# Experts of a mixture layer in plain fp32 on 32-column tiles of the array, instead of three fp32r products of split operands

## The reference, cut to what matters

```python
def swiglu(h, w_gu, w_down):
    gt, up = jnp.split(h @ w_gu, 2, axis=-1)
    return (jax.nn.silu(gt) * up) @ w_down

def moe(h, w_r, b_r, w_gu, w_down):
    t = h.reshape(-1, shp[-1])
    logits = (t @ w_r).astype(jnp.float32) + b_r.astype(jnp.float32)
    top_v, top_i = lax.top_k(logits, TOP_K)
    wts = jax.nn.softmax(top_v, axis=-1)
    comb = jnp.sum(jax.nn.one_hot(top_i, N_EXPERTS, dtype=jnp.float32) * wts[..., None], axis=1)
    for e in range(N_EXPERTS):
        out = out + comb[:, e:e + 1] * swiglu(t, w_gu[e], w_down[e])
```

## Time and profile before

| | us |
|---|---|
| median of 3 runs | 1981.36 (1981.35 to 1981.62) |
| the profiled execution | 1976.57 |
| its span | 1974.4 |
| first product of expert 0 to the end of expert 7 in it | 942.2 to 1950.1 |

### The profile page before, as it was taken

The page is one execution under the profiler, slowest core; times in us unless marked ns, Lnnn a source line. Parts: engine busy times, 40 slices in busy tenths (PEclk is TensorE's granted clock), DMA queues, the critical chain, the costliest instruction groups (busy, mean ns, idle before and its releaser), DMA issues.

```text
span 1974.4 us, 33543 instructions
## 1 busy us (share of the span) xinstructions
PE 1923.0 (97%) x12982; PEld 1627.6 (82%) x12982; DVE 1565.5 (79%) x2210; ACT 1135.9 (58%) x1385; POOL 239.6 (12%) x279
## 2 busy tenths in 40 slices
PE   7999999999998999999999999999999999999997
PEld 3778998899997778988888888888888888888885
DVE  5896457655674976287999989989899898998995
ACT  2214344545432243344777877877778777777774
POOL 2550422000006332340000000000000000000000
PEclk9999999999999999999999999999999999999998
DMA  9576345555552664444799999999999999999993
GB/s 351 186 285 236 131 159 181 196 181 182 179 174 69 203 222 141 167 150 153 269 363 365 353 323 349 368 359 357 324 342 363 365 352 343 334 363 371 345 346 119
DMA packets 143063, 524.12 MB, mean 265 GB/s; under 512 B 16192, under 2 KB 16704, under 8 KB 142272
## 3 DMA queue, kind: packets, MB, share of 16 engines
q1 hardware_dynamic: 140544, 508.82, 71.3%
q10 hardware_dynamic: 1728, 7.90, 1.2%
q0 software_dynamic: 640, 5.35, 0.7%
HBM read 515.57 MB, written 6.43 MB: 264 GB/s over the span
## 4 chain that ended last, share of the span: by engine, by line
PE 85%; DVE 10%; ACT 3%; issue 2%; DMA 1%; ACTq 0%; DVEq 0%
PE bank L1044 28%; PE bank L1069 14%; PE bank L882 12%; PE bank L291 9%; PE bank L622 8%; PE bank L486 4%; DVE wlo L2417 3%; PE bank L502 2%; PE bank L969 2%; PE bank L1031 1%; ACT whi L1411 1%; DVE arena L1581 1%; PE bank L451 1%; PE bank L428 1%; DMA masks<-in_masks 1%
## 5 line engine op out<-in xcount | busy, mean ns | idle before, releaser
L2417 DVE TENSOR_TENSOR wlo<-ring,whi 128x1024 fp32r<-128x1024 f32 x756 | 910.4, 1222 | 144.8 <-ACT whi L1411 142.9
L1411 ACT ACTIVATE whi<-ring 128x1024 fp32r<-128x1024 f32 x756 | 799.9, 1060 | 293.2 <-PE bank L1044 145.3
L1044 PE MATMUL bank<-whi,gh 128*128 128x512 f32 x896 | 285.6, 400 | 2.2 <-DVE wlo L2417 0.9
L1044 PE MATMUL bank<-whi,gl 128*128 128x512 f32 x896 | 279.6, 393 | 0.0
L1044 PE MATMUL bank<-wlo,gh 128*128 128x512 f32 x896 | 278.8, 392 | 0.0
L291 PE MATMUL bank<-hT,ring 128*128 128x264 f32 x864 | 204.3, 396 | 5.0 <-issue 3.0
L1044 PEld LDWEIGHTS bank<-wlo,gh 128*128 128x128 f32 x896 | 168.2, 188 | 38.9
L291 PEld LDWEIGHTS bank<-hT,ring 128*128 128x128 f32 x864 | 165.9, 195 | 40.7 <-issue 11.9
L1044 PEld LDWEIGHTS bank<-whi,gl 128*128 128x128 f32 x896 | 168.1, 188 | 38.0
L1044 PEld LDWEIGHTS bank<-whi,gh 128*128 128x128 f32 x896 | 159.6, 188 | 32.3 <-DVE wlo L2417 3.2
L1069 PE MATMUL bank<-whi,eh 128*128 128x512 f32 x448 | 142.5, 399 | 0.3
(11 more groups left out here) (431 smaller groups left out, 3068.6 us busy)
## 6 DMA issues: line engine op xcount, KB each, us to landing
ring<-in_w SPq DMA_DIRECT2D x964, 512.0 KB, 5.2
out_gdns<-arena POOLq DMA_DIRECT2D x2, 2048.0 KB, 8.4
arena<-in_gdn ACTq DMA_DIRECT2D x2, 1536.0 KB, 7.2
xT<-in_x ACTq DMA_DIRECT2D x1, 1056.0 KB, 8.9
out_y<-hT SPq DMA_DIRECT2D x4, 264.0 KB, 2.1
arena<-in_gdn ACTq DMA_DIRECT2D x2, 512.0 KB, 3.8
masks<-in_masks ACTq DMA_DIRECT2D x1, 512.0 KB, 11.0
cpk<-in_cpk SPq DMA_DIRECT2D x1, 512.0 KB, 6.4
```

The lines of the kernel that those rows point to most:

```text
L1044: ins = pe.matmul(o[half], x[:, k, mine], w[part][:, CH * half:CH * half + CH], start=k == 0 and n == 0, stop=k == KD - 1 and n == 2)
L1411: act.activation(whi[:, m % SPL, :], ring[:, r, :], ACT.Copy).then_inc(sem("hi_done"), 1)
L2417: v.tensor_tensor(wlo[:, m % SPL, :], ring[:, (low.base + m) % RING, :], whi[:, m % SPL, :].bitcast(F32), ALU.subtract).then_inc(sem("lo_d ...
```

## The change

Experts keep at most 96 tokens, in three tiles of 32. Their products are plain fp32, so nothing is split: `high` and `low` of expert slots go, and so do `gl` and `el`. For a slot, 12 products of 32 stationary columns and 256 streaming columns are made, in three rounds `r` of four array tiles `j`. Three tokens' tiles times four quarters of the slot's 1024 columns are 12 pairs: array tile `j` below 3 takes tokens `j` and quarter `r`, array tile 3 takes tokens `r` and quarter 3. Round `r` writes bank `3 * (c % 2) + r` upward and bank `3 + r` downward.

The freed room of `whi` and `wlo` becomes seven more places for slots (`ring2`), 14 in all, and SP waits for `e_used`, which PE raises with the last product of a slot. The rows of a chunk are turned by products of 32 stationary columns with the unit matrix, 12 a chunk, into one bank (6). The downward result is first brought together in `ys` by three copies on ACT and three on DVE, since a token tile's last quarter lies on other partitions. The gather has 192 columns, and both parts of `hth` and `htl` accumulate into one bank; only ACT copies it out, to `gx`. Two `combine` follow each of the slots 4 to 7. Further, some loads share semaphores, and POOL clears `yh` and `yl` once.

The core of the diff (expert parts only):

```diff
-CAP = 128
+CAP = 96
-NCH = FF // CH
+NCH = FT // 4
+ERING = 14
+TT = CAP // 32
+DQ = D // 4
...
+        ring2 = over("ring2", [P, ERING - RING, SLOT * P], where(whi), 0, F32)
...
-        ROWS = 2
-        COMBINE = range(3, 11)
-        DCT = 11
+        TURN = 3
+        ROWS = 0
+        COMBINE = range(4, 8)
+        DCT = 9
...
+        def quarter(j, r):
+            return (j, r) if j < TT else (r, TT)
...
                     for m in (2 * i, 2 * i + 1):
-                        for part, src in enumerate((hth, htl)):
-                            for t in range(3):
-                                ins = pe.matmul(bank[2 * (i % sets) + part][:, PAIR * (m % 2):PAIR * (m % 2) + PAIR],
-                                                src[:, t, m * P:(m + 1) * P], dsel[:, t, :], start=t == 0, stop=t == 2)
+                        for t in range(3):
+                            for src in (hth, htl):
+                                ins = pe.matmul(bank[6 + i % 2][:, PAIR * (m % 2):PAIR * (m % 2) + PAIR],
+                                                src[:, t, m * P:(m + 1) * P], dsel[:, t, :], start=t == 0 and src is hth,
+                                                stop=t == 2 and src is htl)
...
+                def slot_products(s, x, first, last):
+                    w = place(s)
+                    for r in range(TT):
+                        for j in range(4):
+                            t, c = quarter(j, r)
+                            o = up_bank(s // KD, r) if s < UP_S else down_bank(r)
+                            ins = pe.matmul(o[32 * j:32 * j + 32, 0:DQ], x(t), w[:, DQ * c:DQ * c + DQ],
+                                            start=first, stop=last)
+                    ins.then_inc(sem("e_used"), 1)
...
-                    for t in range(CH // P):
-                        ins = pe.transpose(bank[4 + c % 2][:, CAP * t:CAP * t + CAP], erow[0:CAP, c % 2, t * P:(t + 1) * P],
-                                           ident[0:CAP, 0:CAP])
+                    for r in range(TT):
+                        for j in range(4):
+                            ins = pe.matmul(bank[6][32 * j:32 * j + 32, P * r:P * r + P],
+                                            erow[:, c % 2, r, 32 * j:32 * j + 32], ident, start=True, stop=True)
...
-                    w = [t[:, s % SPL, :] for t in (whi, wlo)]
-                    o = [bank[2 * (c % 2) + half][0:CAP, :] for half in range(2)]
-                    for n, (x, part) in enumerate(((gh, 0), (gh, 1), (gl, 0))):
-                        for half in range(2):
-                            ins = pe.matmul(o[half], x[:, k, mine], w[part][:, CH * half:CH * half + CH],
-                                            start=k == 0 and n == 0, stop=k == KD - 1 and n == 2)
+                    slot_products(s, lambda t: gx[:, k, mine + 32 * t:mine + 32 * t + 32], k == 0, k == KD - 1)
...
-                    sp.wait_ge(sem("lo_done"), q * FFN_S + (FFN_S + s - RING + 1))
-                    r = (MIX1_END + s) % RING
-                    sp.dma_start(ring[:, r, :], w_in[e * FFN_S + (MIX1_END + s)]).then_inc(landed[r], 16)
+                    if not (s0 and s < ERING):
+                        sp.wait_ge(sem("e_used"), q * FFN_S + (s - ERING + 1))
+                    sp.dma_start(place(s), w_in[e * FFN_S + (MIX1_END + s)]).then_inc(place_sem(s), 16)
...
-                        high(n % RING, q * (16 * FFN_S // RING) + 16 * (n // RING + 1), m, q * FFN_S + (FFN_S + m + 1))
...
-                        low(m, q * FFN_S + (FFN_S + m + 1))
```

More of the change, by code:

```diff
@@ L268, in trunk_program @@
         landed = [sem(f"landed{r}") for r in range(RING)]
+        landed2 = [sem(f"landed2_{r}") for r in range(ERING - RING)]
         used = sem("slots_used")
@@ new lines, in expert @@
+                for f in range(FT):
+                    s, c, i = UP_S + f, f // 4, f % 4
+                    pe.wait_ge(place_sem(s), place_count(q, s))
+                    if f == 0:
+                        pe.wait_ge(sem("dcT_done"), q * 1 + 1)
+                    if i == 0:
+                        pe.wait_ge(sem("turned_done"), q * NCH + (c + 1))
+                    at = lambda t: P * i + 32 * t if i < TT else P * t + CAP
+                    slot_products(s, lambda t: ea[:, c, at(t):at(t) + 32], f == 0, f == FT - 1)
+                    if f == TURN:
@@ L2194, in mixer @@
                         out_low(8 + m)
-                    if l and m >= KD - LAG:
-                        low(m - (KD - LAG), FFN_S + m - (KD - LAG) + 1)
             def residual(src, at, done, mod, tiles=range(KD)):
@@ L2295, in choose, with rows, low @@
                     ins.then_inc(sem("dsel_done"), 1)
-                def gathered(self, i, pg, sets=2):
-                    v.wait_ge(sem("gather_full"), pg * 4 + (i + 1))
-                    v.tensor_copy(gl[:, 2 * i:2 * i + 2, :], both(bank[2 * (i % sets) + 1])).then_inc(sem("gl_done"), 1)
-                def rows(self, g):
+                def rows(self, g, q, a):
+                    v.wait_ge(sem("ywt_done"), g + 1)
+                    if a is not None or q:
+                        v.wait_ge(sem("e_used"), q * FFN_S)
+                    for r in range(TT):
+                        ins = v.tensor_copy(ys[32 * r:32 * r + 32, TT * DQ:D], down_bank(r)[CAP:P, 0:DQ])
+                    ins.then_inc(sem("e_ys"), 1)
+                def low(self, g):
                     for half in range(2):
@@ L2330, in end @@
                 def end(self, g, a):
-                    self.rows(g)
+                    self.rows(g, a * NE + NE, a)
+                    self.low(g)
                     for m in range(KD):
@@ L2359, in finish @@
                 def finish(self, g):
-                    self.rows(g)
+                    self.rows(g, NE, None)
+                    self.low(g)
                     xs, e, gate = self.samples()
@@ L2376, in __call__ @@
                     expert(self, q, g, pg, e, sub, a)
-            four = lambda b: b[:, 0:4 * CAP].rearrange("p (a b) -> p a b", b=CAP)
             def expert(self, q, g, pg, e, sub, a):
                 for m in range(FFN_S):
-                    if not (a is None and e == 0 and m < LAG):
-                        low(m, q * FFN_S + (FFN_S + m + 1))
-                    for c in silu_after(m):
+                    if m == ROWS:
+                        self.rows(g, q, a)
+                        self.low(g)
@@ L2488, in _ @@
             residual(down, 40, "x_ffn", mods[:, 0], range(done, KD))
-            low.base = MIX1_END
             mixer(1)
```

251 lines of the change are left out of this document (121 added, 130 removed).

## The result

The changed kernel takes 1935.87 us (median of 4 runs, 1932.47 to 1937.08), the kernel before beside it 1981.49 (4 runs, 1981.35 to 1981.70). The ratio is 0.9767, with a 95% interval of 0.9750 to 0.9784: 45.6 us or 2.3% faster, where 39.0 us were forecast. The profiled execution of the changed kernel took 1932.47 us with a span of 1930.4, so between the two profiled executions lie 44.1 us.

What follows compares the result with a forecast made beforehand. PE was taken to set the pace, busy for 97% of the span. The terms -64.5 + 17.6 + 10.1 - 0.4 - 1.8 make -39.0 us, from 1981.4 to 1942; own range 1925 to 1975, with rival 1 1928 to 1998.

Steps and rivals of the forecast that it cites:

- slot: Expert slots on PE: twelve plain fp32 products take 1.31 us instead of 1.406, over 672 slots 64.5 us saved.
- turns: Turning a chunk's rows on PE: 0.675 us instead of 0.36, 56 times, 17.6 us added.
- changes of tiling, and `dcT`: Switches between 128 and 32 columns on PE: 56 pairs at 0.18, 10.1 us added; dcT transposes keep their price.
- gather products: The gather's 192 products on PE: 192 columns instead of 256, 0.115 us instead of 0.117, a gain of 0.4 us.
- stage: The expert stage: 1007.9 us become 970.7 after slots, turns, changes of tiling and gather products.
- start and end: Before and behind the expert slots: earlier norm, first slot needing one gathered part, later copies into ys; together -1.8 us.
- The norm of the experts' input: At the mixer's end: without two waits for low (1.14 + 1.15 us) the norm starts about 2.2 us earlier.
- The copies into `ys`: Behind expert 7: three copies of 256 columns stand in front of ACT's work, 1.2 us later.
- Rival 1: Gather on PE: 192-column fp32r products cost plain fp32's 0.332 us, 51.6 us added instead of 0.4 gained; chance 0.28.
- Rival 2: Between slots on PE: waits cost a change of tiling, 0.09 us x 672 = 60, so 2002 us; chance 0.07.
- Rival 3: Weight transfers in the stage: no more than 351 GB/s, 1004 us for the stage, about 1975; chance 0.05.
- The rule that spoke against it: Slot rounds on PE: the skill's 3.07 times for four packed tiles, not four; the prediction set it aside for plain fp32.

Runs made afterwards that it cites:

- four_rounds: Changed kernel with a fourth round in every expert slot, the third round's four products done twice: 2226.4 us (one run).
- dve_turns: Changed kernel with the turns moved from TensorE to VectorE's own 32x32 transposes, down weights' rows reordered to suit: 1900.59 us, ratio to the kernel before 0.9597.
- combine8: Changed kernel with an expert's eight combines behind eight slots, one each, and the dcT transposes behind slot 13 instead of 9: 1947.07 us, ratio 0.9832.
- bunched: dve_turns with combines behind two slots, four each, dcT transposes right after, and a gather's four parts behind one slot: 1890.18 us, ratio to the kernel before 0.9535.
- last_gather: bunched without the unused gather behind expert 7 (one product and one copy stay in its place): 1881.59 us, ratio to the kernel before 0.9505.
- two_rounds: Changed kernel without the third of the three rounds of products in every expert slot, all weights still transferred: 1836.5 us, ratio to the kernel before 0.9274.
- tile_by_tile: Changed kernel with a slot's two product loops swapped, three products of each array tile in a row: 2375.4 us (one run).

## Why the prediction was right, and where it was off

The mechanism was right: PE set the pace before and after, and the change was a sum of starts on PE. Measured were 45.6 us for the 39.0 of the forecast. The terms, with what they measured:

| term | forecast | measured | from |
|---|---|---|---|
| slot | 1.406 to 1.31: -64.5 | 1.297: 672 x 1.297 = 871.6 for 945: -73.4 | timeline, four_rounds |
| turns | +17.6 | 56 x (0.66 - 0.36) = +16.8 | timeline, dve_turns |
| changes of tiling, and `dcT` | 56 x 0.18 = +10.1, its transposes unchanged | 32 x 0.323 + 16 x 0.296 = +15.1; `dcT` 8 x 0.626 = 5.0 against 4: +1.0 | timeline, combine8, bunched |
| gather products | -0.4 | 192 x 0.1125 = 21.6 against 22.5: -0.9 | timeline, last_gather |
| stage | -37.2 | -42.9 (the terms make -41.4; 1.5 are not accounted for) | 1007.9 to 965.0 |
| start and end | -1.8 | +0.7 and -1.8 | below |

**The mis-sized term is the slot's**: 8.9 us too little saved, where the total is off by 6.6. I had drawn a line through a round of 128 columns (0.225) and one of 512 (0.86). In the stage the turns show 0.218 for a round of 128 columns (0.655 / 3) and the slots 0.432 for 256. Half of the long row, 0.43, was thus right, and the short row, which stands between other work, was 0.007 too long and pulled the line to 0.437; at 0.0044 in each of 2016 rounds that is 8.9 us. I had taken half of the long row as my lower bound and chosen the line over it. Part of the error was given back by the second one: a change of tiling costs 0.30 to 0.33 and not 0.18, since I had read it from two rows with 512-column products behind it and then taken off something for a first load. That is 6 us too little cost there (with the 1.0 of `dcT`), against 9 too little saving in the slots; that the two errors have opposite signs is luck.

**Start.** The norm of the experts' input was to start 2.2 us earlier. In the timeline, which answers to the earlier trace rows, DVE has no `low` any more between the residual of tile 7 and the norm (line 1574), and waits for PE's sum of squares (line 434) alone:

```profile
913.86 3.72 PE L434 MATMUL bank<-slab,ones 128*128 128x264 f32 x16
...
914.05 0.17 DVE L2231 TENSOR_TENSOR tmp<-bank,mods 128x8 f32<-128x8 f32 x1 [1.99 <-PE bank L653]
...
914.91 0.23 DVE L1593 SCALAR_TENSOR_TENSOR mods<-mods,cols 128x72 f32<-128x72 f32 x1
...
917.69 0.43 DVE L1574 TENSOR_SCALAR tmp<-bank 128x264 f32<-128x264 f32 x1 [2.55 <-PE bank L434]
```

The same two places in the kernel before:

```profile
911.57 3.72 PE L403 MATMUL bank<-slab,ones 128*128 128x264 f32 x16
...
916.74 0.43 DVE L1544 TENSOR_SCALAR tmp<-bank 128x264 f32<-128x264 f32 x1
```

From the start of PE's sum to the norm are 3.83 us, where they were 5.17: the missing `low`s saved 1.34 us of the 2.2. The sum itself takes as long in both kernels, so the first of the two waits, in front of the residual of tile 7, had not been on the path. All of it is nevertheless 2.3 us later than before (913.86 for 911.57), and the clock may say why: in 865 to 880 us it was granted 0.66 in this execution, and 0.97 in that of the kernel before.

```profile
865.00:880.00 15.00, 14.63 (x64) 10.34 (x63) 12.50 (x17) 4.96 (x7) 10.84 (x6) 0.66 0.11 36
```

The first slot starts 0.20 us behind the last gather product and no longer waits for all parts, as forecast. But the first gather ran longer at the lower clock (granted 0.72 in 930 to 942 us, before 0.86), and that took most of it back. So the first slot starts at 942.86 for 942.19.

**End.** The copies into `ys` were forecast at +1.2. From the last slot's end at 1907.88 to the first placing product at 1910.80 are 2.9 us, where the earlier trace rows have 1.5: +1.4. The rest went the other way. PE's last sum of squares took 3.83 us and before 6.81, with a granted clock of 1.00 where before it was 0.55, in these executions, so that the tail as a whole was 1.8 us shorter. No step of the forecast stands behind that: that start and end came near the -1.8 together is luck.

**The rivals.** Rival 1 had 0.28 and was refuted by the rows of the gathers in the stage: products of 192 columns cost 0.11 us. last_gather confirms it. The chance was too high: 8 and 256 columns at nearly the same price in the earlier trace rows leave little room for a peak between them. Rival 2 (waits between slots cost a change of tiling) falls with four_rounds and the 1.297, in which every wait is contained. Rival 3 falls with 362 to 372 GB/s in the stage's stretches and the 404 to 408 of two_rounds. The adds did not hold up the `dcT` transposes: they start 2.73 us behind the last `combine`'s change back (1073.80 to 1076.53), which is two slots and the start into the full width. PE's idle time in the stage, SP's waits for PE and the full clock came out as forecast, and so did the price of an expert: 84 x 1.297 + 7 x 0.66 + 4 x 0.823 + 0.626 = 117.5 us without a gather and 4 x 1.646 more with one, 124.1, where I had 118.2 and 124.5; from first slot to first slot the trace has 117.3 and 123.9.

**The rule that spoke against it.** A round of four tiles takes 0.432 us, and one product of full width with as many columns, by the 1.73 ns of the earlier trace rows, 0.443. Packing by four costs nothing here. The Trainium skill ("TensorE: Matmul & The Clock Gate", section "Measured speedup vs the span model") has 3.07 times instead of four, for four tiles packed by rows of the array (K = 32); for four tiles packed by columns, as here, it has no row, which the prediction did not say. By the 3.07 a round would be 4 / 3.07 of a single product, some 0.58 us, a slot 1.73, and the kernel slower by the 290 us of four_rounds less the 46 gained, an estimate by that page. Carried over to column tiles it does not hold in this trace, while tile_by_tile shows that an order with the same tiles can lose 30% of the rate (1.85 us a slot).

## What to carry to other kernels

When PE sets the pace, count its starts by columns and by changes of tiling, and check the sum against one interval between equal places of a steady stretch, not against a short row between other work. An engine that has become free (here DVE at 39%) is the place for what is left on PE beside the products: the turns on DVE gave 35 us, beside the 46 of the change itself. Full-width work between 32-column products belongs together, at 0.3 us for each change and back; and before a rewrite that frees transfers, a run with a part of the products left out tells how far the transfers' floor lies below.

## What the runs showed of the hardware

- Four plain fp32 products on four 32-column tiles of 256 columns start within 20 ns of each other, and the next four records follow after 0.216 us; a round takes 0.432 us, as long as one full-width product of 256 columns (0.443 by the 1.73 ns a column of the earlier trace rows).
- The four tiles do not keep the queue's order among each other: products of a turn started before those of the slot ahead of them. With three products in a row for one tile a slot takes 1.85 us instead of 1.297.
- A change between full width and 32-column tiles and back costs 0.30 to 0.33 us with fp32r products of 192 or 264 columns, in three parts: 0.14 into the full width, 0.10 before the second full-width product, 0.09 back.
- fp32r products of 192 columns cost 0.1125 us at the full clock, next to 0.117 for 256 and 0.11 for 8 columns.
- A core took in weights at 404 to 408 GB/s from 1000 to 1780 us of two_rounds, without a break.
- DVE turned a 128x128 fp32 tile by 32x32 blocks in 284 ns, which is what its product of two such tiles takes (283).
